# The end of a two-layer encoder trunk with tokens on partitions: residual rows stored ahead of the router, last pass combined by products, final norm by accumulated squares

## What is computed

```python
def _rmsnorm(x, g):
    xf = x.astype(jnp.float32)
    xf = xf * lax.rsqrt(jnp.mean(xf * xf, axis=-1, keepdims=True) + EPS)
    return xf.astype(x.dtype) * g

def _moe_swiglu(h, w_router, b_router, w_exp_in, w_exp_out):
    logits = (h @ w_router).astype(jnp.float32) + b_router
    top_val, top_idx = lax.top_k(logits, TOP_K_EXPERTS)       # 2 of 8
    top_w = jax.nn.softmax(top_val, axis=-1)
    combine = jnp.sum(jax.nn.one_hot(top_idx, N_EXPERTS) * top_w[..., None], axis=-2)
    out = jnp.zeros_like(h)
    for e in range(N_EXPERTS):
        out = out + combine[..., e:e + 1] * _swiglu(h, w_exp_in[e], w_exp_out[e])
    return out

# layer 1, then the end; gate_f has one vector for the prompt, one for the stream
h = _rmsnorm(x, p["g_norm_ffn"][l]) * (1 + scale_f) + shift_f
x = x + gate_f * _moe_swiglu(h, ...)
y = _rmsnorm(x, p["g_final"])
```

## Time and profile before

| | |
|---|---|
| median of three executions | 1528.15 us |
| the profiled execution, in all | 1528.08 us |
| its span, first to last instruction | 1526.3 us |
| PE busy | 1414.5 us (93%) |
| DVE, ACT, POOL busy | 1024.2, 783.3, 40.3 us |
| share of PE in the chain that ended last | 88% |
| mean granted TensorE clock | 0.958 of 2.4 GHz |
| moved by DMA | 327.33 MB |

### The profile page before, as it was taken

How to read it: one execution, slowest core, us unless ns; L and a number is a source line. 1 busy time by engine, 2 the same in 40 slices (tenths; PEclk the granted TensorE clock), 3 DMA queues, 4 the chain that set the end, 5 groups by cost and what they waited for, 6 DMA issues and landing times.

```text
span 1526.3 us, 24618 instructions
## 1 busy us (share of the span) xinstructions
PE 1414.5 (93%) x9375; PEld 1253.1 (82%) x9375; DVE 1024.2 (67%) x1417; ACT 783.3 (51%) x1059; POOL 40.3 (3%) x66
## 2 busy tenths in 40 slices
PE   5899999998889999998999999987999999999984
PEld 4788998875889999997999988766788888888863
DVE  1476998775454444425879886644588988889855
ACT  1534447634433333225444675243477887878752
POOL 0000100000000000000001000000200000000100
PEclk8899999999989999999999999998699999999996
DMA  9856743124446877435767651246389999999952
GB/s 288 216 178 200 236 141 121 60 83 152 141 132 200 247 228 240 163 89 146 228 195 254 209 151 53 96 134 227 116 309 384 384 383 388 378 386 385 383 208 67
DMA packets 280084, 327.33 MB, mean 214 GB/s; under 512 B 32304, under 2 KB 190456, under 8 KB 279992
## 3 DMA queue, kind: packets, MB, share of 16 engines
q1 hardware_dynamic: 273042, 314.29, 62.0%
q10 hardware_dynamic: 5478, 6.53, 1.2%
q0 software_dynamic: 1472, 5.24, 1.0%
HBM read 310.84 MB, written 15.17 MB: 214 GB/s over the span
## 4 chain that ended last, share of the span: by engine, by line
PE 88%; DVE 5%; ACT 2%; DMA 2%; issue 2%; ACTq 1%; SPq 0%; POOLq 0%; DVEq 0%; POOL 0%
PE mmp L804 14%; PE mmp L806 13%; PE mmp L805 13%; PE mmp L1202 8%; PE mmp L1204 8%; PE mmp L1203 8%; PE mmp L798 7%; PE px L854 2%; PE py L774 2%; PE py L870 2%; PE px L774 1%; PE lg L969 1%; PE lg L774 1%; PE px L1011 1%; DVE hT L1772 1%
## 5 line engine op out<-in xcount | busy, mean ns | idle before, releaser
L804 PE MATMUL mmp<-hT_hi,wm_hi 128*128 128x320 f32 (+1 forms) x976 | 308.4, 316 | 11.1 <-issue 5.8
L806 PE MATMUL mmp<-hT_hi,ring_lo 128*128 128x320 f32 (+1 forms) x976 | 306.1, 314 | 0.0
L805 PE MATMUL mmp<-hT_lo,wm_hi 128*128 128x320 f32 (+1 forms) x848 | 263.9, 311 | 0.0
L1803 DVE TENSOR_TENSOR ring_lo<-ring,wm_hi 128x1024 fp32r<-128x1024 f32 (+1 forms) x124 | 148.2, 1201 | 93.1 <-ACT wm_hi L1408 90.7
L804 PEld LDWEIGHTS mmp<-hT_hi,wm_hi 128*128 128x128 f32 (+1 forms) x976 | 184.8, 189 | 16.5 <-issue 8.9
L806 PEld LDWEIGHTS mmp<-hT_hi,ring_lo 128*128 128x128 f32 (+1 forms) x976 | 184.6, 189 | 0.2
L1408 ACT CAST wm_hi<-ring 128x1024 fp32r<-128x1024 f32 (+1 forms) x124 | 126.6, 1028 | 96.9 <-PE mmp L806 78.4
L805 PEld LDWEIGHTS mmp<-hT_lo,wm_hi 128*128 128x128 f32 (+1 forms) x848 | 160.1, 189 | 0.1
L1363 ACT ACTIVATE tmp<-mmp 128x320 f32<-128x320 f32 x70 | 30.6, 438 | 233.8 <-PE mmp L806 164.7
L1891 DVE SCALAR_TENSOR_TENSOR conv<-u_conf,dwc,conv 128x350 f32<-128x350 f32 x240 | 132.2, 582 | 3.1
L804 PE MATMUL mmp<-h_hi,wd_hi 128*128 128x320 f32 x352 | 111.3, 316 | 8.8 <-DVE h_lo L2050 8.8
(11 more groups left out here) (364 smaller groups left out, 2893.8 us busy)
## 6 DMA issues: line engine op xcount, KB each, us to landing
ring<-in_w_in_dram SPq DMA_DIRECT2D x104, 512.0 KB, 4.5
ring<-in_w_exp_in_dram SPq DMA_DIRECT2D x64, 512.0 KB, 8.1
more<-in_w_exp_in_dram SPq DMA_DIRECT2D x64, 512.0 KB, 11.3
ring<-in_w_ada_dram SPq DMA_DIRECT2D x56, 512.0 KB, 6.9
more<-in_w_exp_out_dram SPq DMA_DIRECT2D x48, 512.0 KB, 5.5
ring<-in_w_ffn_in_dram SPq DMA_DIRECT2D x44, 512.0 KB, 5.9
wide<-in_w_ada_dram SPq DMA_DIRECT2D x40, 512.0 KB, 7.5
ring<-in_w_branch_dram SPq DMA_DIRECT2D x48, 256.0 KB, 2.8
```

What stands on the lines that cost most here:

```text
L804: nc.tensor.matmul(out, w_hi, x_hi, start=is_first, stop=False)
L805: nc.tensor.matmul(out, w_hi, x_lo, start=False, stop=False)
L806: return nc.tensor.matmul(out, w_lo, x_hi, start=False, stop=is_last)
L1803: V.tensor_tensor(mix_rows(ring_lo, l, s, r), mix_rows(ring, l, s, r), mix_hi(l, s, r).bitcast(F32), ALU.subtract).then_inc(mix_lo_ready, 1)
```

## The change

The result of the experts is combined with tokens on partitions, and `xT` is no longer updated in layer 1's second half.

- **Ahead of the router** TensorE turns `xT` to rows (24 transposes, L1203 of the new file), ACT copies them to `y_late` in six copies around the scaling of `hT`, and SP stores them in `x_dram`. In layer 1's gate stage SP stores the feed-forward gate, 16 columns of 128 elements, in `gate_dram`.
- **At the first pass** DVE builds one-hot matrices `Sz`, which hold the late weight of each token whose late row lies in the last pass; that weight is taken out of `w_ab[1]`. TensorE turns `Sz`, ACT copies it to `SzT` (the memory of `std`). `S0` moves to `y`.
- **In the last pass** POOL loads the late rows directly behind the early ones. ACT scales the early rows after the last pass's chunk 15. SP loads the prompt's gate, spread to 128 partitions, among the last weights, and behind them the rows of x, the final gain and the stream's gate.
- **At the end** DVE forms x + gate * (early + late) on rows, multiplies the last pass's result by each gate from PSUM, TensorE makes six products with `SzT`, DVE adds, ACT squares with an accumulated sum and takes the root, DVE scales, and SP stores.

```diff
@@ SP, gate stage @@
+                        if l and j == 8:
+                            sp.wait_ge(mods_added, DEPTH * ADA_PAIRS)
+                            for s_ in range(2):
+                                for c in range(DC):
+                                    sp.dma_start(gate_dram[s_, c * P:(c + 1) * P].unsqueeze(1),
+                                                 mods[:, l, 40 + c, s_:s_ + 1]).then_inc(gate_stored, 16)
@@ SP, loads of the first pass @@
+                        if k == MSLOTS - 1:
+                            for t in range(3):
+                                m = P if t < 2 else TS
+                                sp.wait_ge(x_copied, 2 * (t + 1))
+                                sp.dma_start(x_dram[t * P:t * P + m, :], y_late[0:m, t, :]).then_inc(x_stored, 16)
@@ SP, last pass and end @@
+                            if k == MSLOTS + 2 and is_last:
+                                sp.wait_ge(xg_done, p + 1)
+                                sp.wait_ge(gate_stored, 16 * 2 * DC)
+                                sp.dma_start(gate_rows[0][:], gate_dram[0:1, :].broadcast_to([P, D])
+                                             ).then_inc(gate_loaded, 16)
...
+                    sp.wait_ge(chunk_done, last * CPP + (n0 + 12))
+                    sp.dma_start(x_end[:, 0:2, :], x_dram[0:2 * P, :].rearrange("(t p) d -> p t d", p=P)
+                                 ).then_inc(end_loaded, 16)
+                    sp.dma_start(x_end[0:TS, 2, :], x_dram[2 * P:T, :]).then_inc(end_loaded, 16)
+                    sp.dma_start(fin_rows, g_final.unsqueeze(0).broadcast_to([P, D])).then_inc(end_loaded, 16)
+                    sp.wait_ge(chunk_done, last * CPP + (n0 + 13))
+                    sp.dma_start(gate_rows[1], gate_dram[1:2, :].broadcast_to([P, D])).then_inc(end_loaded, 16)
+                    for t in range(3):
+                        sp.wait_ge(out_ready, t + 1)
...
@@ POOL @@
             for c, (dst, landed) in enumerate(((x_tok, early_rows), (y_late, late_rows))):
-                if c == 1:
-                    pool.wait_ge(y_saved, last * 16 + 16)
-                    nc.gpsimd.sem_inc(y_free, 1)
@@ PE, first pass and end @@
+                    pe.wait_ge(sz_ready, 1)
+                    for t in range(3):
+                        ins = nc.tensor.transpose(py[:, t * P:t * P + rows[t]], Sz[0:rows[t], t, :],
+                                                  ident[0:rows[t], 0:rows[t]])
+                    ins.then_inc(sz_tr, 1)
...
+                    pe.wait_ge(szT_ready, 1)
                     for t in range(3):
+                        for h in range(2):
+                            pe.wait_ge(y_gated_ready, h + 1 if t < 2 else 3)
+                            c = slice(h * 512, (h + 1) * 512)
+                            ins = nc.tensor.matmul(z_banks(t)[0:rows[t], c], SzT[:, t * P:t * P + rows[t]],
+                                                   y_gated[t // 2][:, c], start=True, stop=True)
+                        ins.then_inc(z_done, 1)
@@ ACT, end @@
-            norm(4, lambda c: vec[:, 0, R_GFIN + c:R_GFIN + c + 1], lambda c: None)
...
+                        act.wait_ge(z_added, t + 1)
+                        nc.scalar.activation(z_banks(t)[0:m, :], y_late[0:m, t, :], ACT.Square,
+                                             accum_out=sum_sq[0:m, t, :]).then_inc(z_squared, 1)
+                        act.wait_ge(z_squared, t + 1)
+                        nc.scalar.activation(root[0:m, t, :], sum_sq[0:m, t, :], ACT.Sqrt, scale=1.0 / D,
+                                             bias=eps[0:m, 0:1]).then_inc(root_ready, 1)
@@ DVE, end @@
+                    dve.wait_ge(gate_loaded, 16)
+                    dve.wait_ge(end_loaded, 16 * 4)
+                    for t in range(3):
+                        ins = V.tensor_tensor(y_late[0:m, t, :], y_late[0:m, t, :], gate_rows[t // 2][0:m, :], ALU.mult)
...
+                        ins = V.tensor_tensor(y_late[0:m, t, :], y_late[0:m, t, :], x_end[0:m, t, :], ALU.add)
...
+                    for h in range(2):
+                        V.tensor_tensor(y_gated[0][:, c], mmp[:, 2 + h, :], gate_rows[0][:, c],
+                                        ALU.mult).then_inc(y_gated_ready, 1)
+                    V.tensor_tensor(y_gated[1], mmp[:, 2:4, :].rearrange("p a b -> p (a b)"), gate_rows[1],
+                                    ALU.mult).then_inc(y_gated_ready, 1)
...
+                    add_z(0)
+                    add_z(1)
+                    end_row(0)
+                    add_z(2)
+                    end_row(1)
+                    end_row(2)
```

More of the change, by code:

```diff
@@ L279, in build @@
         xrow = eb("xrow", [P, D])
-        small = eb("small", [P, 448])
+        small = eb("small", [P, 480])
         y_late = eb("y_late", [P, 3, D])
@@ L319, in build @@
         gap, w_top, w_ab, swap, row_0 = table(3), table(2, 3), table(2, 3), table(2, 3), table(3, 1)
-        S0 = y_late[:, 0, 0:3 * P].rearrange("p (t s) -> p t s", t=3)
+        row_z, in_z, w_z, row_end = table(3, 1), table(3, 1), table(3, 1), table(1)
+        sum_sq, root, r_root = table(3, 1), table(3, 1), table(3, 1)
+        assert table_at[0] <= 480
+        S0 = y[:, 0:3 * P].rearrange("p (t s) -> p t s", t=3)
+        Sz = y[:, 3 * P:6 * P].rearrange("p (t s) -> p t s", t=3)
+        SzT = std
+        y_gated = (y, hid_tok[:, 0:D])
+        end_flat = ring[:, :, :].rearrange("p a b -> p (a b)")
+        x_end = end_flat[:, 0:3 * D].rearrange("p (t d) -> p t d", t=3)
+        fin_rows = end_flat[:, 3 * D:4 * D]
+        gate_rows = (xrow, end_flat[:, 4 * D:5 * D])
         rows_dram = nc.dram_tensor("rows_dram", (NP * P, D), F32).ap()
+        x_dram = nc.dram_tensor("x_dram", (T, D), F32).ap()
+        gate_dram = nc.dram_tensor("gate_dram", (2, D), F32).ap()
         def we_hi(k):
@@ L1140, in _ @@
                 else:
+                    pe.wait_ge(x_ready, DC // 2 * (2 * l + 2))
+                    pe.wait_ge(pair_evac, pair_no["out", l, 3] + 1)
+                    for t in range(3):
+                        m = P if t < 2 else TS
+                        for c in range(DC):
+                            ins = nc.tensor.transpose(x_banks(t)[0:m, c * P:(c + 1) * P], xT[:, c, t * P:t * P + m],
+                                                      ident[:])
+                            if c % 4 == 3:
+                                ins.then_inc(x_tr, 1)
                     for c in range(DC):
@@ L1606, in _, with x_copy @@
                 else:
-                    norm(2 * l + 1, gain_of(1), shift_of(1), pairs=(3,))
+                    def x_copy(b):
+                        t, g = b // 2, b % 2
+                        m = P if t < 2 else TS
+                        c = slice(g * 512, (g + 1) * 512)
+                        act.wait_ge(x_tr, b + 1)
+                        copy(y_late[0:m, t, c], x_banks(t)[0:m, c]).then_inc(x_copied, 1)
+                    square(2 * l + 1, 3)
+                    norm_std(2 * l + 1)
+                    for b in range(3):
+                        x_copy(b)
+                    norm_scale(2 * l + 1, gain_of(1), shift_of(1))
+                    for b in range(3, 6):
+                        x_copy(b)
                     act.wait_ge(stored, 16 * 10 * DEPTH)
@@ L1642, in _ @@
                             gathered()
+                            act.wait_ge(sz_tr, 1)
+                            copy(SzT[:], py[:, 0:T]).then_inc(szT_ready, 1)
                         high(k)
@@ L1666, in run_pass @@
                                 gathered()
-                            if k == CPP - 1:
+                            if k == 15 and is_last:
+                                act.wait_ge(ab_ready, 1)
+                                act.wait_ge(early_rows, 16 * 3)
+                                for t in range(3):
+                                    m = P if t < 2 else TS
+                                    nc.scalar.activation(x_tok[0:m, t, :], x_tok[0:m, t, :], ACT.Copy,
+                                                         scale=w_ab[0:m, 0, t:t + 1]).then_inc(early_scaled, 1)
+                            if k == CPP - 1 and not is_last:
                                 act.wait_ge(y_free, p + 1)
@@ L2165, in low_hid @@
                                         ALU.subtract).then_inc(hidT_split, 1)
-                    for k in range(AHEAD):
-                        if k == AHEAD - 2:
-                            low_gathered(1)
+                    for k in range(AHEAD - 2):
                         low(k)
@@ L2218, in _ @@
-            norm(4)
-            for b in range(6):
-                t, g = b // 2, b % 2
-                m = P if t < 2 else TS
-                dve.wait_ge(y_tr, b + 1)
-                V.tensor_copy(x_tok[0:m, t, g * 512:(g + 1) * 512], mmp[0:m, b % 4, :]).then_inc(y_copied, 1)
+                        ins = V.scalar_tensor_tensor(y_late[0:m, t, :], y_late[0:m, t, :], w_ab[0:m, 1, t:t + 1],
```

(13 more changed lines are left out.)

93 lines of the change are left out of this document (47 added, 46 removed).

## The result

The changed kernel takes 1520.70 us (median of six executions, 1518.99 to 1523.06), the kernel before, timed beside it, 1528.46 (1525.71 to 1529.91): a ratio of 0.9947, 95% interval 0.9932 to 0.9962. It is faster, by 8 us, where 18.6 were forecast; 1520.7 lies above the upper end of the range. The profiled execution took 1519.65, its span is 1517.9 (before: 1526.3).

What follows compares the result with a forecast made beforehand. It took the sparse 44.8 us tail after TensorE's last expert matmul as the room to gain. The new tail, walked to 1507.3, plus 0.4 around the router gave span 1507.7, 18.6 less than before: 1509.5 us, range 1505 to 1513.

Steps and rivals of the forecast that it cites:

- Sixteen gate stores: Layer 1's gate stage: SP issues them in 8.8 of 9.0 us of waiting, so they cost nothing.
- second rival: Gate stage: the sixteen small stores clog the ring ahead of the weights, 8 us more, 1518; chance 0.07.
- it ends at 1479.5 in place of 1476.5: DVE's last weight subtraction, last pass: slips 3.0 us as late rows and a gate row delay the last weights to 1475.3.
- Passes: Expert passes up to the last pass but one: forecast at +0.
- Around the router: Small DVE operations before the first pass take 3.9 us against 3.5 of waiting: 0.4 us delay.
- The turning of x: Transposes and copies before the router, claimed hidden in idle time; rival: not hidden, up to 7 us more, chance 0.04.
- fourth rival: Router: the clock stays up and its 10.2 us halve, 5 us less, 1504.5; chance 0.09.
- Products: Tail: six fp32 matmuls on TensorE at half clock, 1.7 us per 512 columns, 3.4 for the first pair.
- Gate and residual: Tail: six DVE operations of 1024 columns on rows, 7.0 us, the largest new term.
- Loads for the end: x rows, final gain and second gate row behind the last weights land by 1482.3, just covered.
- Norm and store: Tail: additions, square, table load, root, scaling to 1504.0, then 3.3 us of store, ending at 1507.3.
- signs of being wrong: DMA wait before gate product; last five chunks' casts waiting with TensorE gap; gap near 885; end above 1516 or below 1502.

Runs made afterwards that it cites:

- A: Changed kernel with the sixteen gate stores moved behind the x stores, where SP is idle: 1514.00 us, ratio 0.9912 to the kernel before.
- D: Changed kernel with gate stores moved, the prompt's gate row behind the last weights and late rows held until the last pass's chunk 12: 1514.54 us, ratio 0.9918.
- B: Changed kernel with the prompt's gate row loaded behind the last weights, first of the loads of the end: 1519.87 us, ratio 0.9951.
- E: A with DVE's three gated products of the last pass ahead of the additions of x: 1511.05 us, ratio 0.9895.
- W: A with the 24 transposes of hT issued twice, ahead of the loop over the passes: 1520.79 us, one execution.
- L: K with the loads of the end in order of need, a semaphore for each: 1509.16 us, ratio 0.9877.
- K: E with a square root ahead of the tail on ACT and the third product added before the first row block is scaled: 1510.42 us, ratio 0.9888.

## Why the prediction was wrong

- **"Sixteen gate stores ... At the 0.55 of its issue there they take 8.8 us of 9.0: nothing."** This is the first step that failed. SP was held 13.9 us and the engines longer, and 2.6 to 6.7 us reached TensorE (A). The prediction had it as its second rival and gave it a chance of 0.07, with no row of a store this small to lean on. The Trainium skill (DMA: Bandwidth & Descriptors, Specifications) says that the engine reads, modifies and writes below 512 B. No run here shows that step itself, but the cost it hints at came, and it should have moved the stores to where SP is idle, or the forecast by some of the 8 us.
- **"it ends at 1479.5 in place of 1476.5."** The mechanism was right, the size was not: 4.7 us of slip in place of 3.0. I added 5.5 us to the landing and set 2.5 against it as slack. The slack was there, the landing was mis-sized: the last weights landed at 1485.1, which is 1476.9 without the 8.2 us of the last pass's late start, so 7.1 us were added in place of 5.5, and the last cast waits for its DMA. The last load was issued at 1473.2, where 1461.5 and the 8.2 us make 1469.7. D, without the two transfers, has no slip. B to D show too that moving them only moves the wait.
- **Passes**: costed at nothing, without a reason, and 1.8 us in the profile (1.4 to 1.5 in A to E). No row of before shows it.
- **Around the router, 0.4 us**: 0.5 in every variant but W. The turning of x is hidden, as said. The 3.3 us beyond it are of the profiled execution's clock, and their cause is open. My fourth rival, a router at full clock, did not come: 10.22 us throughout.
- **"Products ... At that level ... 3.4 for the first pair"**: 3.75 at half clock, as chosen (the 0.54 that it starts from is the 0.34 of the earlier trace rows and the 0.20 before it). **Gate and residual, 7.0**: 7.0 from 1492.97 to 1499.98. **Loads for the end "just covered"**: no wait there, but with the gate row at the end (B) 2 us. **Norm and store**: from the first addition on 13.1 us (1504.82 to 1517.9) against 13.0. There is luck in it: the forecast had the second pair out of the way, and it was not; it came level with the root.

The tail, the largest part of the argument, was right within 0.8 us of 28. Of the 10.2 us missed in the profile, the new transfers ahead of it made 4.2 (stores 2.55, slip 1.68); the clock around the router made 3.3 and the passes 1.8, both with open cause. A, without the stores in the gate stage, closes the account better: over the same intervals its profile is 3.7 us above the forecast, 1.5 of slip, 1.4 of passes, 0.75 of tail and 0.1 around the router, and its median is 4.5 above 1509.5. Of the prediction's own signs of being wrong three came: a gap near 885 (in SP's loads), casts that wait for their DMA with a pause on TensorE (5.84 us for chunk 13, though only 0.24 and 0.64 among the last five), and an end above 1516. The change keeps 8 of the 18.6 us; with the stores in another place it is 13 to 14, and with the tail's order (L) 19.

## What to carry to other kernels

A store of one element per partition costs the queue and the engines by its pieces, not by its bytes; put it where the queue is idle, however small it is. Where the DMA engines are full to the end, as here, a transfer put among the last weights delays them (here by more than its bytes at the full rate), and reordering moved the wait without shortening it. A stall of the busiest engine is worth nothing if the chain that ends last does not pass through it: read the chain first, and test the stall by moving it.

## What the hardware showed unexpectedly

TensorE's clock at the first pair of products, with its idle time before them, in the timelines of K, of E and of L:

```profile
1490.87 1.96 PE L1326 MATMUL lg<-y,std 128*128 128x512 f32 x4 [2.34 <-DVE y L2306]
```
```profile
1491.29 2.60 PE L1326 MATMUL lg<-y,std 128*128 128x512 f32 x4 [2.92 <-DVE y L2305]
```
```profile
1490.42 3.75 PE L1326 MATMUL lg<-y,std 128*128 128x512 f32 x4 [4.30 <-DVE y L2305]
```

In these three, after 2.3 us of idleness the pair took 1.96 us, at full clock (1.00 over 1488 to 1492 in K), after 4.3 it took 3.75, and after 2.9 it took 2.60. And ACT's squares need no table of their own here: behind the root's table load in K they ran with no further load, which takes 1.28 us out of such a norm for the price of one activation in idle time.
